# Keeping split weights in HBM between two uses, for a two-layer recurrent decoder step

## What is computed

```python
for layer in range(2):
    hn = rmsnorm(x, norm_mix[layer])
    mix = mixer_even(...) if layer % 2 == 0 else mixer_odd(...)   # h @ w_in, chunked recurrences, @ w_out
    x = x + mix
    h = rmsnorm(x, norm_ffn[layer])
    g, u = split(h @ w_up)            # 1024 -> 2 * 2816
    x = x + (silu(g) * u) @ w_down    # 2816 -> 1024
y = rmsnorm(x, norm_final)
```

## Time and profile before

| | |
|---|---|
| median of three runs | 2495.21 us (2494.74 to 2500.96) |
| the profiled execution | 2493.78 us, span 2492.0 us |
| TensorE (PE) busy | 2432.9 us, 98% of the span |
| POOL, DVE, ACT busy | 1252.7, 1007.6, 934.2 us (50, 40, 37%) |
| `wl` subtractions on POOL | 392, 943.3 us busy |
| `wh` copies on ACT | 396, 410.0 us busy |
| mean granted TensorE clock | 0.992 of full speed |
| moved by DMA | 235.18 MB, mean 94 GB/s; HBM read 221.64 MB, written 9.05 MB |

### The profile page before, as it was taken

How to read it: one execution, slowest core, us unless ns; L and a number is a source line. 1 busy time by engine, 2 the same in 40 slices (tenths; PEclk the granted TensorE clock), 3 DMA queues, 4 the chain that set the end, 5 groups by cost and what they waited for, 6 DMA issues and landing times.

```text
span 2492.0 us, 36702 instructions
## 1 busy us (share of the span) xinstructions
PE 2432.9 (98%) x15510; PEld 2193.5 (88%) x15510; DVE 1007.6 (40%) x1712; ACT 934.2 (37%) x1219; POOL 1252.7 (50%) x669
## 2 busy tenths in 40 slices
PE   8999999899999999999999999999999999999998
PEld 6889987688887877999999889988887889999998
DVE  4513245334445434543333443454434454222224
ACT  5342345233223455443333254544432335222223
POOL 3745455555455644544354473344445556544453
PEclk9999999999999999999999999999999999999999
DMA  5322233321323222222222222222233323222222
GB/s 184 102 82 69 71 130 97 115 77 60 123 85 119 92 90 92 88 74 94 85 77 94 77 88 87 85 95 75 86 101 107 126 86 127 92 88 93 94 85 86
DMA packets 74594, 235.18 MB, mean 94 GB/s; under 512 B 9216, under 2 KB 13120, under 8 KB 74432
## 3 DMA queue, kind: packets, MB, share of 16 engines
q1 hardware_dynamic: 74432, 232.84, 27.9%
HBM read 221.64 MB, written 9.05 MB: 93 GB/s over the span
## 4 chain that ended last, share of the span: by engine, by line
PE 86%; DVE 5%; POOL 2%; issue 2%; ACT 2%; POOLq 1%; DVEq 1%; DMA 1%; SPq 0%; ACTq 0%
PE ps L761 62%; PE ps L816 17%; POOL wl L1380 1%; DMA wr<-in_wblk 1%; PE ps L912 1%; PE ps L910 1%; PE ps L856 1%; ACT wh L1114 1%; PE ps L785 0%; DVE sq L1550 0%; DVE mixl L1764 0%; POOL sq L1486 0%; PE ps L973 0%; POOLq L1397 0%; PE ps L970 0%
## 5 line engine op out<-in xcount | busy, mean ns | idle before, releaser
L1380 POOL TENSOR_TENSOR wl<-wr,wh 128x1024 fp32r<-128x1024 f32 x392 | 943.3, 2420 | 592.2 <-ACT wh L1114 591.7
L761 PE MATMUL ps<-xh,wh 128*128 128x260 f32 (+2 forms) x3296 | 882.5, 322 | 8.1 <-DVE qk L1552 4.2
L761 PE MATMUL ps<-xl,wh 128*128 128x260 f32 (+2 forms) x3296 | 869.0, 318 | 0.0
L761 PE MATMUL ps<-xh,wl 128*128 128x260 f32 (+1 forms) x3280 | 867.1, 319 | 0.0
L761 PEld LDWEIGHTS ps<-xh,wh 128*128 128x128 f32 (+1 forms) x3296 | 544.4, 188 | 61.6 <-issue 18.8
L761 PEld LDWEIGHTS ps<-xl,wh 128*128 128x128 f32 (+1 forms) x3296 | 543.7, 188 | 44.9 <-issue 2.4
L761 PEld LDWEIGHTS ps<-xh,wl 128*128 128x128 f32 x3280 | 541.9, 188 | 44.6
L1114 ACT ACTIVATE wh<-wr 128x1024 fp32r<-128x1024 f32 (+2 forms) x396 | 410.0, 1045 | 393.8 <-DMA wr<-in_wblk 389.2
L816 PE MATMUL ps<-hidh,wh 128*128 128x260 f32 (+1 forms) x1024 | 279.9, 327 | 21.8 <-POOL wl L1380 9.5
L1239 ACT ACTIVATE sq<-sq 128x512 f32<-128x512 f32 (+1 forms) x88 | 55.9, 636 | 609.0 <-DVE sq L1550 609.0
L816 PE MATMUL ps<-hidl,wh 128*128 128x260 f32 (+1 forms) x1024 | 276.3, 323 | 0.0
(11 more groups left out here) (373 smaller groups left out, 2316.9 us busy)
## 6 DMA issues: line engine op xcount, KB each, us to landing
wr<-in_wblk SPq DMA_DIRECT2D x392, 512.0 KB, 3.4
xr<-in_xT SPq DMA_DIRECT2D x8, 260.0 KB, 5.8
xB<-in_xT SPq DMA_DIRECT2D x8, 260.0 KB, 5.8
out_yT<-xB SPq DMA_DIRECT2D x8, 260.0 KB, 2.2
xr<-in_xT SPq DMA_DIRECT2D x8, 256.0 KB, 6.0
xA<-in_xT SPq DMA_DIRECT2D x8, 256.0 KB, 4.4
Ss<-in_s_even SPq DMA_DIRECT2D x1, 2048.0 KB, 10.1
out_ss_even<-Ss SPq DMA_DIRECT2D x1, 2048.0 KB, 9.2
```

The costliest lines, as they stand in the source:

```text
L761: mm = pe.matmul(ps[0:cols, b + c, 0:n], wt[:, w], xt[:, e:e + n], start=first, stop=end)
L1380: pool.tensor_tensor(lo, raw, hi.bitcast(F32), ALU.subtract).then_inc(s_lo, 1)
```

## The change

A block's high and low part are written to HBM after its first use has been prepared, and for the second use both parts are read back, with no copy on ACT and no subtraction on POOL.

- `Plan` marks which uses are the second (`second`), counts for each use what the semaphores will hold (`loads`, `splits`, `stores`), and puts an item `("ws", n - 2)` behind `("w", n)` if n - 2 is a first use.
- ACT, at `("ws", n)`, waits until `wh` and `wl` of block n are there and issues two stores of 512 KB from its own queue.
- SP, at `("w", n)`, waits as before for the end of the last use of n - 4 and also until the stores of block n - 4 have landed. A second use is then two loads of 512 KB, one in `wh` and one in `wl`.
- TensorE waits, for a second use, for the two loads alone.
- POOL's subtraction for a first use is done as two instructions of 128 x 512, one after the other.

```diff
+        for n, s in enumerate(self.blocks):
+            at[n % 4] += 32 if self.second[n] else 16
+            self.loads[n] = at[n % 4]
+            split += not self.second[n]
+            self.splits[n] = split
+            if n in self.kept:
+                stored[n % 4] += 32
+            self.stores[n] = stored[n % 4]
+        kept, items = set(self.kept), []
+        for x in out:
+            items.append(x)
+            if x[0] == "w" and x[1] > 2 and x[1] - 2 in kept:
+                items.append(("ws", x[1] - 2))
...
             def weights(n):
                 if n >= 4:
                     sp.wait_ge(s_unit, pl.end[n - 4] + 1)
+                    ge(sp, s_ws[n % 4], pl.stores[n - 4])
                 s = pl.blocks[n]
+                if pl.second[n]:
+                    sp.dma_start(wh[n % 4][:].bitcast(F32), a["split"][s, 0]).then_inc(s_w[n % 4], 16)
+                    sp.dma_start(wl[n % 4][:].bitcast(F32), a["split"][s, 1]).then_inc(s_w[n % 4], 16)
+                    return
...
             def weights_ready(u):
                 for n in pl.blk[u]:
-                    pe.wait_ge(s_hi, n + 1)
+                    if pl.second[n]:
+                        pe.wait_ge(s_w[n % 4], pl.loads[n])
+                        continue
+                    pe.wait_ge(s_hi, pl.splits[n])
...
             def weights_hi(n):
+                if pl.second[n]:
+                    return
                 w = block_cols(n)
-                act.wait_ge(s_w[n % 4], 16 * (n // 4 + 1))
+                act.wait_ge(s_w[n % 4], pl.loads[n])
...
+            def store(n):
+                act.wait_ge(s_hi, pl.splits[n])
+                if n < 3:
+                    act.wait_ge(s_lod, n + 1)
+                else:
+                    act.wait_ge(s_lo, pl.splits[n] - 3)
+                s = pl.blocks[n]
+                act.dma_start(a["split"][s, 0], wh[n % 4][:].bitcast(F32)).then_inc(s_ws[n % 4], 16)
+                act.dma_start(a["split"][s, 1], wl[n % 4][:].bitcast(F32)).then_inc(s_ws[n % 4], 16)
...
             def weights_lo(n):
-                if n < 3:
+                if n < 3 or pl.second[n]:
                     return
...
-                pool.tensor_tensor(lo, raw, hi.bitcast(F32), ALU.subtract).then_inc(s_lo, 1)
+                    pool.tensor_tensor(lo, raw, hi.bitcast(F32), ALU.subtract).then_inc(s_lo, 1)
+                    return
+                for e in (slice(0, w // 2), slice(w // 2, w)):
+                    last = pool.tensor_tensor(lo[:, e], raw[:, e], hi[:, e].bitcast(F32), ALU.subtract)
+                last.then_inc(s_lo, 1)
```

More of the change, by code:

```diff
@@ L355, in __init__ @@
                 out.extend(after.get(self.u[x], ()))
-        self.items = out
+        seen, self.second = set(), {}
+        for n, s in enumerate(self.blocks):
+            self.second[n] = s in seen and not isinstance(s, tuple)
+            seen.add(s)
+        self.again = [n for n in self.second if self.second[n]]
+        self.kept = [n for n, s in enumerate(self.blocks) if not self.second[n] and not isinstance(s, tuple)]
+        self.loads, self.splits, self.stores, at, split = {}, {}, {}, [0] * 4, 0
+        stored = [0] * 4
+        for n, s in enumerate(self.blocks):
+            at[n % 4] += 32 if self.second[n] else 16
[10 more added lines that the diff above has]
+                items.append(("ws", x[1] - 2))
+        self.items = items
+        out = items
         assert sum(1 for x in out if x[0] == "w") == len(self.blocks)
@@ L495, in build @@
         s_w = [sem(f"w{s}") for s in range(4)]
+        s_ws = [sem(f"ws{s}") for s in range(4)]
         x_in = [sem(f"x_in{m}") for m in range(KT)]
@@ L713, in _ @@
                     final_half(v[0])
+            for s in range(4):
+                sp.wait_ge(s_ws[s], pl.stores[len(pl.blocks) - 4 + (s - len(pl.blocks)) % 4])
             sp.wait_ge(s_st0, 16)
@@ L734, in weights_ready @@
                     else:
-                        pe.wait_ge(s_lo, n - 2)
+                        pe.wait_ge(s_lo, pl.splits[n] - 3)
             def x_tile_ready(n, k):
@@ L1322, in _ @@
                     weights_hi(v[0])
+                elif k == "ws":
+                    store(v[0])
                 elif k == "x0":
@@ L1372, in weights_lo @@
             def weights_lo(n):
-                if n < 3:
+                if n < 3 or pl.second[n]:
                     return
                 w = block_cols(n)
-                pool.wait_ge(s_hi, n + 1)
+                pool.wait_ge(s_hi, pl.splits[n])
                 raw, hi, lo = wr[n % 4][:, 0:w], wh[n % 4][:, 0:w], wl[n % 4][:, 0:w]
@@ L2274 @@
     o = {k: nc.dram_tensor(f"out_{k}", shape, F32, kind="ExternalOutput").ap() for k, shape in _OUTS.items()}
+    a["split"] = nc.dram_tensor("split", (arrays["in_wblk"].shape[0], 2, P, D), F32).ap()
     build(nc, a, o)
```

## The result

The changed kernel takes 2529.67 us (2528.1 to 2532.47, four runs), the kernel before beside it 2495.89: a ratio of 1.0137, 95% interval 1.0125 to 1.0149. It is slower by 34 us where 9 were forecast.

What follows compares the result with a forecast made beforehand. TensorE, busy for 98% of the span, was taken as the bound. 2493.8 - 7.2 - 5.1 + 6.5 + 11.7 + 1.6 + 3.4 = 2504.7, then + 1.4 - 0.9 = 2505 us; range 2480 to 2530.

Steps and rivals of the forecast that it cites:

- the four gains: TensorE waits at 165, 824, 1374 and 1549 us shrink as copies and subtractions go; sum 7.2 us, before clock dips.
- 824 us step: At 824 us ACT's copy for a second use goes, shortening TensorE's wait for VectorE; gain 2.3 us.
- 1374 us step: At 1374 us two POOL subtractions that held up VectorE's go; gain 2.0 us.
- 1549 us step: At 1549 us ACT's copy leaves the chain of ACT and VectorE, VectorE's scan remains; gain 1.0 us.
- 165 us step: At 165 us POOL's products start earlier without a second use's subtraction, ACT's exponentials late next; gain 1.9 us.
- The projections: In `in` and `out`, the loop load, copy, store, load takes 9.2 us and may take 10.9; taken as no loss.
- rival 3: Projections fall behind by their load and store loop, TensorE waiting in `in`; 13 us more, 2518 us; chance 0.07.
- d1 and d2 in the four dense groups: Block A: d1's load waits for u0's store, so d1 and d2 are ready late; 1.5 us in one group, sum 6.5.
- The three groups with 2 MB: At 672, 748 and 1867 us late d1 and d2 meet 2 MB transfers; losses 5.0, 3.2 and 3.5, sum 11.7 us.
- The clock: Two old dips go (5.1 us) and half a third (0.9); two of three new waits dip, costing 3.4.
- Rival 2: Landing decides everywhere: store pair and the load behind it take 3 us longer together; 2532 us; chance 0.15.
- Rival 1: The relief wins: d1 lands early enough, nothing lost there or at the 2 MB transfers; 2483 us; chance 0.2.

Runs made afterwards that it cites:

- e6: Changed kernel, with second uses among 26 to 131 (projections) loaded raw and split again, their blocks not stored; 2516.62 us, ratio 1.0086.
- e4: Kernel before, with POOL's subtractions in two halves and nothing else; 2493.43 us, ratio 0.9990.
- e12: Kernel before, nothing stored, POOL's subtraction in halves only for uses 156 to 255; 2492.09 us, ratio 0.9984.
- e7: Changed kernel, stores one block earlier, only 15 second uses read back (124, 125, 209 to 216, 236 to 240); 2494.80 us, ratio 0.9993.
- e9: Changed kernel, stores one block earlier, only 30 second uses read back (26 to 29, 124, 125, 232 to 255); 2483.40 us, ratio 0.9949.
- e1: Changed kernel, with ACT issuing each block's stores one block earlier; 2509.97 us, ratio 1.0059.
- e3: Changed kernel, with only one block stored and every second use reading that block back; 2479.61 us, ratio 0.9933.
- e8: Changed kernel, stores one block earlier, only the low part stored and read back, ACT remaking the high part; 2498.56 us, ratio 1.0014.
- e5: Changed kernel, with the 2 MB load of layer 1's states and the two stores ahead of it three steps later; 2520.17 us, ratio 1.0095.
- e2: Changed kernel with all its stores, but second uses loaded raw and split again, nothing read back; 2542.94 us, ratio 1.0188.
- e11: e9 with POOL's subtraction in halves only for uses 156 to 255, in one instruction elsewhere; 2483.52 us, ratio 0.9943.

## Why the prediction was wrong

The sign was right; the size was not: +34 us instead of +9. In the forecast idle time grew by 12.6 us (-7.2 + 6.5 + 11.7 + 1.6) and the clock gave 2.6 back; measured are +26.7 and +9.4. So 14 of the missing us are waits and 12 are clock. Two steps failed above all, by about 13 us each: the projections were taken at nothing, and the three groups that meet 2 MB were priced at half of what they cost. By the steps of the prediction:

**Removed, the four gains (forecast 7.2, with dips 13.2).** The 824 us step was right: 2.3 and a dip of 1.7 against 4.8 measured, and e6, which leaves those blocks out, loses most of it. The 1374 us step had the right size (2.0 + 3.4 against 5.0) by a cause half right: e4 and e12 get 3.5 of it with nothing read back. The 1549 us step, taken at 1.0 because "VectorE's scan remains", gave 4.8 (3.3 of idle time and the lower clock behind it): the scan itself was being slowed by POOL, as e7 and e9 show, which the earlier trace rows had shown for another operation and which I didn't carry over. The 165 us step (1.9 and half a dip) failed in the changed kernel and came in e1, e3 and e8 (-1.9 to -3.4). What stood in its place is in the changed kernel's timelines of SP and ACT; the last row is ACT's of the kernel before:

```profile
158.76 0.32 SPq L619 DMA_DIRECT2D wh<-split  x1
...
160.07 0.43 SPq L634 DMA_DIRECT2D EK<-in_ret  x1
...
166.74 1.28 ACT L1244 ACT_TABLE_LOAD   x1 [6.14 <-DMA EK<-in_ret]
```

```profile
154.50 1.28 ACT L1198 ACT_TABLE_LOAD   x1 [0.25 <-DMA EK<-in_ret]
```

The constants `EQ` and `EK`, which ACT's exponentials need, stand in SP's order behind a pair of weight loads, and this pair waited for a store of a first use until 158.76. The constants were issued 7.7 us later than before (159.61 against 151.94), but TensorE itself was 7.3 us later by then, so this is 0.4 us. The rest is the landing: right behind 1 MB of loads, and with stores under way, `EK` landed 6.6 us after its issue instead of 2.1 (before it was issued at 152.31), and the 3.84 us of the earlier trace rows became 6.88. In e1 the pair is issued 5 us ahead of the constants, and `EK` lands after 2.2. I had listed POOL and ACT as what could be late next and had left out SP, although I had written that the new wait is SP's.

**The projections: taken at nothing, cost 13.5 us** (6.6 to 155 us and 6.9 to 420). ACT's timeline of the changed kernel has the copies of consecutive blocks:

```profile
76.87 1.06 ACT L1150 ACTIVATE wh<-wr 128x1024 fp32r<-128x1024 f32 x1 [3.20 <-DMA wr<-in_wblk]
...
84.73 1.06 ACT L1150 ACTIVATE wh<-wr 128x1024 fp32r<-128x1024 f32 x1 [5.49 <-DMA wr<-in_wblk]
...
92.21 1.06 ACT L1150 ACTIVATE wh<-wr 128x1024 fp32r<-128x1024 f32 x1 [5.14 <-DMA wr<-in_wblk]
...
97.13 1.06 ACT L1150 ACTIVATE wh<-wr 128x1024 fp32r<-128x1024 f32 x1 [2.71 <-DMA wr<-in_wblk]
...
103.55 1.06 ACT L1150 ACTIVATE wh<-wr 128x1024 fp32r<-128x1024 f32 x1 [4.21 <-DMA wr<-in_wblk]
```

One round of the loop, load n, store n - 2, load n + 2, is two copies further on: 15.3, 12.4 and 11.3 us, where I reckoned 9.2 and had room for 10.9. The loop itself was the right mechanism; its terms were the landings of a quiet kernel. I added a load of 3.4 to a store pair of 4.3 as if they were alone. In these three rounds the pair landed 5.6, 7.6 and 6.1 us after its first issue and the load after 7.1, 4.7 and 5.1. The medians from 76 to 120 us, 4.7 for a load and 4.9 for a pair's second store, would have fitted into 10.9. The first round has 2.6 us more, which the prediction left out: SP had four small transfers of a rotation to issue ahead of the load, as its timeline shows.

```profile
82.61 2.41 SPq L718 DMA_DIRECT2D T3b<-qk  x4
```

The 9.5 us of cover were used up, and the rest fell on TensorE in small waits of 0.8 to 1.7 us. The price I gave to rival 3, 13 us, was right; its chance, 0.07, was not, and it came on top of the forecast and not in its place. That load n + 2 hangs on the landing of load n at all is the order of ACT's list: e1 takes 2 us off the first stretch and 3 off the second, and e8, which also halves the bytes of the stores, takes nearly all of what is left.

**d1 and d2 in the four dense groups: the mechanism was right, and the sum too (6.5 forecast, 5.9 measured), the single terms were not.** In e1 d1 is issued at u0's end: by its timelines of SP and ACT the last of six issues ends at 771.98 + 30.01 = 801.99, before the Silu for `up 0` begins.

```profile
771.98 30.01 SPq L625 DMA_DIRECT2D wr<-in_wblk  x6
...
802.40 0.63 ACT L1287 ACTIVATE sq<-sq 128x512 f32<-128x512 f32 x1 [10.47 <-DVE sq L1604]
```

In the changed kernel it is issued 4.8 us after u0's end. The prediction said 7, since I let the store wait for the copy ahead of it; but the store was issued while ACT still ran the Silu, before that copy (at 820.41) had even begun. The timelines of ACT, SP, POOL and DVE of the changed kernel, put together in order of time, in the group that is the first of the earlier trace rows, whose u0 ends at 819.1:

```profile
819.87 0.63 ACT L1285 ACTIVATE sq<-sq 128x512 f32<-128x512 f32 x1 [8.55 <-DVE sq L1602]
819.93 0.33 ACTq L1159 DMA_DIRECT2D split<-wh  x1
...
820.41 1.05 ACT L1150 ACTIVATE wh<-wr 128x1024 fp32r<-128x1024 f32 x1
...
823.94 16.85 SPq L623 DMA_DIRECT2D wr<-in_wblk  x4
...
828.53 1.06 ACT L1150 ACTIVATE wh<-wr 128x1024 fp32r<-128x1024 f32 x1 [4.23 <-DMA wr<-in_wblk]
829.67 3.01 POOL L1431 TENSOR_TENSOR wl<-wr,wh 128x512 fp32r<-128x512 f32 x2 [1.87 <-ACT wh L1150]
830.02 1.34 ACT L1278 ACTIVATE mixh<-vm,par 128x520 fp32r<-128x520 f32 x2
830.77 2.47 DVE L1816 SCALAR_TENSOR_TENSOR mixl<-vm,par,mixh 128x520 fp32r<-128x520 f32 x2 [3.51 <-ACT mixh L1278]
833.33 0.69 DVE L1602 TENSOR_TENSOR sq<-ps,rsA 128x512 f32<-128x512 f32 x1
836.00 2.48 POOL L1431 TENSOR_TENSOR wl<-wr,wh 128x512 fp32r<-128x512 f32 x2
```

d1's low part is ready 13.5 us after u0's end (832.68; reckoned 14.7), and still this group loses 3.5 us instead of 1.5: TensorE waits 3.19 us where it waited 1.05 before, and the rest is clock. The late copy of d1 held `mixh` behind it on ACT, and that held DVE's `mixl`. DVE's next `sq` began at 833.33, 14.2 us after u0's end (12.1 before), although u2, which it takes out of PSUM, was over about 10.9 us after it. POOL's multiplication and d2's subtraction follow it. I had followed d1 down POOL's order only; ACT's order was the shorter way to TensorE. The other three dense groups lose 2.4 us together, where some 5 were forecast. In e1 the loss of the first goes from 3.5 to 0.8.

**The three groups with 2 MB: 11.7 forecast, 24.7 measured (18.4 of it idle time).** The orders of SP and, at 672 us, of POOL were the right mechanism; the sizes were half. At 672 us 5.0 stands against 8.5: TensorE waits 3.77 us for `pick` and 2.87 for `wl`, where it waited 0.65 in all before. At 748 us 3.2 stands against 6.4, of which 4.4 is idle time. At 1867 us 3.5 stands against 9.8, of which 8.0 is idle time: d2's load landed 14.8 us after its issue, because a 2 MB load and two stores of states stood ahead of it on its queue, with four of the split's stores on the other. e5 moves that load, and the loss of the whole stretch falls by 11 us. The rest of the 13.6 us there is 0.6 in the next dense group and two dips of the clock of 1.5 each, which no wait of over 2 us precedes. In e1, where d1 is issued at once, the first two of these groups still lose 4.9 and 3.2 us.

**The clock: 2.6 us gained in the forecast, 9.4 lost.** I counted three new waits over 2 us and two dips of 1.7. The changed kernel has five new ones of 2.9 to 8.7 us between 700 and 1911 us, and 6.9 in the place of 3.8 at 165 us, with stretches at half clock around or behind them. This is no cause of its own but a surcharge on the waits: 9.4 on 26.7 in the changed kernel, 16.5 on 32.4 in e2.

**Store against load.** Of the pair issued together the parts land after 3.7 and 4.8 us when stored and after 3.3 and 4.2 when loaded, by the medians; but the stores run beside the loads of first uses, where a single weight load has 4.5. The shortest of 196 are 2.6 and 3.6 us for the stores and 3.1 and 4.0 for the loads, the other way round, as the row of before had it (2.9 us for a store of 512 KB). So no run here shows the rule of the Trainium skill cited in the prediction (page "DMA: Bandwidth & Descriptors", section "Anatomy of one DMA — SWDGE (gpsimd) path"): the medians go with it, the shortest times against it. The 3.5 us that hang on it are a small part of what was missing.

**The rivals.** Rival 2 gave 2532 and came nearest, but that was luck: in the group at 784 us the pair of stores and the load behind it took 8.6 us together (819.93 to 828.53) where I had reckoned 8.4 and the rival 11.4. The loop in the projections, the 2 MB groups and the clock made up the time. Rival 1 is what e3 measured, 2480 against 2483, when the stores are absent.

What is left open: why the clock fell behind the wait near 441 us in every kernel but in the trace of before. This makes up 1.5 of the 2.3 to 2.6 us at 420 to 690 us that even the kernels without stores there lose; e12 has it too and gains 1.0 back at 483 us. Open too is why the wait at 41 us is 1.95 us in e11 and 0.6 in e9.

## What to carry to other kernels

A wait added to the engine that issues the loads delays everything behind it in that engine's order: list every load and constant there, and price the loop that closes over it with landings under the new traffic, not with those of the quiet kernel. An engine at 98% gets nothing from relief elsewhere except at the few places where it waits; the relief of 196 blocks was worth 17 us, and 30 well-chosen blocks gave 12 of it with a sixth of the stores. Where a forecast has new waits of several microseconds, it needs a third to a half as much again for the clock (9.4 on 26.7 us here, 16.5 on 32.4 in e2).

## What the runs showed of the hardware

- ACT's queue issued DMAs while ACT still ran the instruction ahead: the store at 819.93 begins 0.06 us after the Silu of 0.63 us began and 0.48 us before the copy that stands ahead of it in ACT's list, and the copies run on. In the changed kernel the median issue takes 0.33 us, and 0.46 for the second of a pair.
- As far as these rows show, a DVE instruction with two operands from SBUF gets on only when a POOL subtraction ends: 8 columns took 1.15 us in e7, until 1546.66, when POOL's ended at 1546.64, and 0.14 us in e9. One with an operand from PSUM wasn't held: `hf` took 0.68 us in e12 at 1368.51 us, in the midst of a POOL subtraction. The Trainium skill, page "GPSIMD Engine Reference", section "1. Specifications", names this contention for VectorE instructions with two SBUF inputs; the traces agree and give its size. Cutting POOL's instruction in two took a pair on DVE from 5.57 to 3.37 us.
- The clock didn't fall behind every wait: in e1 it fell behind one of 7.4 us and not behind one of 3.7, behind the one of 3.49 us near 441 us it fell in e12 and not in the trace of before, and in the changed kernel two dips near 1960 us had no wait of over 2 us ahead of them.
- With 215 GB/s instead of 94 on the mean a weight load took 4.5 us instead of 3.4 by the median, and the matmuls were no slower at full clock (28 or 29 in 6 us). A load of 512 KB issued right behind one of 2 MB on the same queue landed after 14.8 us.
